# Inverse roots of the norms: a square root on ScalarE and a reciprocal on VectorE in place of a logarithm and an exponential

## The chip, the core and the metric

One core of one Trainium2 chip runs the whole program in one launch. The metric is the device time of an execution in microseconds (us). Engines are named as in the profile: PE is TensorE's matrix multiply and PEld its weight load, DVE is VectorE, ACT is ScalarE, POOL is GpSimd, SP is SyncE, which issues the DMAs.

## What is computed

A sequence of 512 tokens of width 1024 goes through four layers. The first two each hold two branches: an HGRN2 branch (4 heads of 128, chunked gated recurrence) and an RWKV-7 branch (8 heads of 64), merged through gates and an output projection. The last two are a gated linear recurrence (RG-LRU) and a retention layer of 4 heads. Normalisations lie between and inside them. Each needs, per token and group, the inverse root of a mean of squares:

```python
o_hg = o_hg * lax.rsqrt(jnp.mean(jnp.square(o_hg), -1, keepdims=True) + RMS_EPS)   # per HGRN head
y_rw = (y_rw - mu) * lax.rsqrt(var + GN_EPS)                                        # per RWKV head
x = (xf - mu) * lax.rsqrt(var + LN_EPS)                                             # layer norm, twice
y = xf * lax.rsqrt(jnp.mean(xf * xf, axis=-1, keepdims=True) + RMS_EPS)             # RMS norm, four times
out = (out - mu) * lax.rsqrt(var + GN_EPS_2)                                        # per retention head
```

## The kernel before

**Layout.** Activations stand transposed: features on the 128 partitions, the 512 tokens along the columns, so that a width of 1024 is eight tiles of 128x512. Matrix products come close to full fp32 precision by splitting: each activation tile becomes a high part (`act_hi`, a ScalarE copy in `high`, L708) and the rest (`act_lo`, a VectorE subtraction in `low`, L1106), and each block of eight weight tiles a high part (`w_hi`, ScalarE, `weights`, L700) and a low one (`w_lo`, GpSimd, L625). `project` (L1690) then makes three matmuls for every weight tile. Two weight buffers alternate: ScalarE's copy for block b+2 waits until PE has used block b.

**Order of the work.** Every engine's program is written out by hand; engines run their instructions in order and meet at semaphores. Loops of the hardware (`Fori`) run the four HGRN heads of a layer, among others. PSUM banks are shared by a plan of jobs: `job_ready` waits until PE has filled a bank, `job_read` signals that it has been read, `evacuated_job` waits for that signal. A `Chain` counts VectorE's or ScalarE's instructions that have to wait for their own predecessor; in a loop `HG_CHAIN` is the number of such waits per turn.

**Norms.** As tokens lie along the columns, a sum over features is a product with a matrix of ones on PE (`sum_squares`, L1707, or a single matmul), whose result stands on all partitions: one 128x512 tile with a mean of squares for every token. Squares are made by ScalarE (`square`, L715, into two staging tiles, so that from the third on each waits for PE's matmul of the one before the last). Then comes the inverse root, on ScalarE alone:

```python
def inverse_root(dst, job, scale, eps, signal, turn=0):
    x = job_ready(act, job, turn)
    job_read(A(dst, x, ACT.Ln, scale=scale, bias=eps), job)
    evacuated_job(act, job, turn)
    A(dst, dst, ACT.Exp, scale=-0.5).then_inc(signal, 1)
```

VectorE waits for the signal and multiplies (L1109 or L1106). This helper (L720, L722) serves 18 places: the eight HGRN heads (`hg_head`, two layers of four; called at L854), the two layer norms (L960), the four RMS norms (`rms`, L967: `pre0`, `post0`, `pre1`, `post1`), and the four retention heads (L1076). The RWKV group norm of each layer does the same for four tiles at once, four Ln and then four Exp (L935, L938), while VectorE takes them tile by tile: product, gain and bias, bonus, gate, and the split (L1445 to L1452). A table load stands in ScalarE's program wherever the function asked for isn't in the table that is loaded.

**Around the changed places.** Between two HGRN heads ScalarE goes on with the next head's gates (`forget_gate`: two Sigmoids, L810 and L811, and a copy, L813), then the split of the finished head (`high`, L708), then two logarithms (L818, L819), and then a weight copy. VectorE multiplies the head's output by its norm (L1109) and by its gate (L1106), splits it (`low`), and starts on the next head's gates (L1285 on). After the last head both go on to the RWKV chunks, which PE opens by itself. After each retention head but the last two ScalarE's next weight copy comes behind a wait for VectorE's finished products; after the last two the splits come first.

Of the kernel before, what the change touches and what calls it, by code (L numbers as in the profile page):

```python
# [16 lines left out]
ACT = mybir.ActivationFunctionType  # L17

P = 128
T = 512  # L20
D = 1024
# [108 lines left out]

HG_CHAIN = 4

# [169 lines left out]
def build(nc, shapes):  # L302
# [10 lines left out]
    with ExitStack() as ctx:  # L313
        def sb(name, shape, dt=F32):
            return ctx.enter_context(nc.sbuf_tensor(f"{name}_sb", shape, dt))
# [14 lines left out]
        stage = sb("stage", [P, 2, 516])  # L330
        wa = sb("wa", [P, T])
        cond = sb("cond", [P, DEPTH, 24])
        derived = sb("derived", [P, 160])
# [355 lines left out]
        def _(act):  # L689
# [26 lines left out]

            def inverse_root(dst, job, scale, eps, signal, turn=0):

                x = job_ready(act, job, turn)
                job_read(A(dst, x, ACT.Ln, scale=scale, bias=eps), job)  # L720
                evacuated_job(act, job, turn)
                A(dst, dst, ACT.Exp, scale=-0.5).then_inc(signal, 1)  # L722

# [8 lines left out]
            for l in range(DEPTH):  # L732
# [82 lines left out]
                def hg_head(turn, last):  # L815
# [37 lines left out]
                    A(ring[3], x, ACT.Square).then_inc(S("hg_sq"), 1)  # L853
                    inverse_root(scores, ("hg_square", l), 1.0 / P, 1e-6, S("hg_rms"), turn)  # L854
                    if not last:
# [72 lines left out]


                for j in range(QT):  # L930
                    evacuated_job(act, ("gn_mean", l, j))
                    A(R_[:, j, :], P3[:, j, :], ACT.Square).then_inc(S("gn_sq"), 1)
                for j in range(QT):
                    x = job_ready(act, ("gn_var", l, j))
                    job_read(A(K_[:, j, :], x, ACT.Ln, scale=1.0 / 64, bias=64e-5), ("gn_var", l, j))  # L935
                for j in range(QT):
                    evacuated_job(act, ("gn_var", l, j))
                    A(K_[:, j, :], K_[:, j, :], ACT.Exp, scale=-0.5).then_inc(S("gn_rs"), 1)  # L938
                act.wait_ge(block_used, b_gate + 16)
# [12 lines left out]
                for m in range(KT):  # L952
                    weights(b_out + m + 2)
                for m in range(KT):
                    if m < 7:
                        act.wait_ge(S("xc_ready"), 7 * l + m + 1)
                    else:
                        evacuated_job(act, ("ln_mean", l))
                    square(("ln", l), m, xa[:, m, :])
                inverse_root(merged[:, 0, :], ("ln_var", l), 1.0 / D, 1e-5, S("ln_rs"))  # L960


            def rms(key, job, tiles, ready):
                for m in range(KT):
                    ready(m)
                    square(key, m, tiles[:, m, :])
                inverse_root(RS, job, 1.0 / D, 1e-6, S("rms_rs"))  # L967

# [91 lines left out]
            def attend(h):  # L1060
# [9 lines left out]
                for v in range(4):  # L1070
# [4 lines left out]
                    square(("ret", h), v, hg[:, 4 * h + v, :])  # L1075
                inverse_root(RS, ("r_var", h), 1.0 / 512, 1e-5, S("rms_rs"))  # L1076

# [23 lines left out]
        def _(dve):  # L1101
# [9 lines left out]
            def low(n, slot, src, turn=0):  # L1111

                dve.wait_ge(split_hi, n + 1 + turn)
                tt(act_lo[:, slot, :], src, act_hi[:, slot, :].bitcast(F32), ALU.subtract).then_inc(split_lo, 1)

            def spread(ap, n):
# [54 lines left out]
            for l in range(DEPTH):  # L1171
# [105 lines left out]
                with dve.Fori(0, QT) as turn:  # L1277
# [80 lines left out]
                    x = job_ready(dve, ("hg_out", l), turn)  # L1358
                    dve.wait_ge(S("hg_rms"), head + 1)
                    gain = vec[:, bass.ds(vec_at[f"hg_g{l}"][0] + turn, 1)]  # L1360
# [82 lines left out]
                for j in range(QT):  # L1443
                    dve.wait_ge(S("gn_rs"), 4 * l + j + 1)
                    y = P3[:, j, :]  # L1445
                    chain.done(tt(y, y, K_[:, j, :], ALU.mult))
                    chain.done(TS(y, y, V(f"gn_g{l}", j), V(f"gn_b{l}", j), ALU.mult, ALU.add))
# [34 lines left out]
                for m in range(KT):  # L1482
                    evacuated(dve, b_out + m)
                    ins = stt(xa[:, m, :], x, -1.0 / D, xa[:, m, :], ALU.mult, ALU.add)
                    job_read(ins, ("ln_mean", l)) if m == 7 else ins.then_inc(S("xc_ready"), 1)
                dve.wait_ge(S("ln_rs"), l + 1)
                for m in range(KT + 1):
# [7 lines left out]

            def normed(n, pre, count):

                dve.wait_ge(S("rms_rs"), count)
                for m in range(KT):
# [6 lines left out]

            def onto_x(n, post, count, x_in, done):

                dve.wait_ge(S("rms_rs"), count)
                dve.wait_ge(S("x_in"), x_in)  # L1510
# [7 lines left out]

            normed(SPLITS["lru_h"], "pre0", 1)
            with dve.Fori(0, RT // 4) as turn:  # L1520
# [64 lines left out]
            for m in (6, 7):  # L1585
                left(dve, LRU_OUT + m)
            onto_x(0, "post0", 2, 64, S("x_done"))
            dve.wait_ge(S("x_done"), 3 * KT)


            normed(SPLITS["ret_h"], "pre1", 3)

# [19 lines left out]
            def attend(h):  # L1612
# [20 lines left out]
                for v in range(4):  # L1633
                    y = hg[:, 4 * h + v, :]
                    ins = stt(y, x, -1.0 / 512, y, ALU.mult, ALU.add)
                    job_read(ins, ("r_mean", h)) if v == 3 else ins.then_inc(S("ret_c"), 1)
                dve.wait_ge(S("rms_rs"), 4 + h)
                for v in range(4):
# [25 lines left out]
            for m in (6, 7):  # L1664
                evacuated(dve, RET_OUT + KT + m)
            onto_x(1, "post1", 8, 80, S("x_final"))

# [563 lines left out]
```

## Time and profile before

| | us |
|---|---|
| three runs: median (lowest to highest) | 2222.09 (2217.86 to 2224.73) |
| the profiled execution, its own time | 2224.56 |
| its span, first to last instruction | 2222.8 |
| PE busy | 1934.4 |
| VectorE busy | 962.9 |
| ScalarE busy | 869.0 |
| GpSimd busy | 607.8 |

The profiled execution's time is 1.8 us above its span. Its mean granted TensorE clock was 0.955 of full speed. Busy times overlap, and a busy PE is not PE at its peak. In a timeline a row gives the start and the length in us, the engine, the line of the kernel (often that of a helper), the operation with its tiles, and in brackets how long the engine had stood idle and whose end released it.

### The profile page before, as it was taken

To read this page: it belongs to the slowest core of one execution; us is meant where nothing else is said; L and a number is where in the kernel's file an instruction comes from. 1 tells how busy PE (TensorE), PEld (TensorE's weight loads), DVE (VectorE), ACT (ScalarE), POOL (GpSimd) and SP (SyncE) were. 2 spreads that over 40 slices of the span, in tenths; PEclk is the share of its full clock that TensorE was granted. 3 is DMA by queue.
4 is the path that set the end of the run, shared out by engine and by line. 5 is a ranking of instruction groups with operands and counts; after the bars stand their busy time and mean duration, and the time that the engine had idled before them with its cause. 6 is when DMAs were issued, how large, how long until landed. Compare 5 with 4: busy or idle time off the path is not lost.

```text
span 2222.8 us, 35507 instructions
## 1 busy us (share of the span) xinstructions
PE 1934.4 (87%) x14368; PEld 1534.2 (69%) x14368; DVE 962.9 (43%) x1299; ACT 869.0 (39%) x1244; POOL 607.8 (27%) x255
## 2 busy tenths in 40 slices
PE   1999988899787998988899797989597998998987
PEld 1876877798565866877798574865474886777755
DVE  5326375632456126375632434737604123232232
ACT  1333456433323334456433324256515323333322
POOL 0333422200252433422300231422141441322212
PEclk9999999999898999999999899999799999999999
DMA  8232222200364322222200323211132231212112
GB/s 333 84 101 64 93 86 71 67 4 13 127 261 156 104 68 67 90 85 71 67 4 13 133 95 133 95 57 48 61 101 95 95 99 43 86 47 66 56 58 77
DMA packets 57524, 192.80 MB, mean 87 GB/s; under 512 B 5408, under 2 KB 5664, under 8 KB 54976
## 3 DMA queue, kind: packets, MB, share of 16 engines
q1 hardware_dynamic: 57408, 191.10, 25.5%
q8 instruction: 92, 1.51, 0.3%
q14 instruction: 24, 0.20, 0.0%
HBM read 173.25 MB, written 17.83 MB: 86 GB/s over the span
## 4 chain that ended last, share of the span: by engine, by line
issue 51%; PE 29%; POOL 9%; DVE 5%; ACT 3%; DMA 1%; POOLq 0%; DVEq 0%; ACTq 0%; SPq 0%
PE proj L1690 17%; POOL w_lo_sb L625 9%; PE aux L1850 2%; PE aux L1781 2%; DVE area_sb L1106 2%; DMA slots_sb<-w_ada 1%; PE aux L1907 1%; PE proj L1850 1%; PE aux L1904 1%; DVE area_sb L1109 1%; DVE slots_sb L1109 1%; ACT L720 1%; DVE act_lo_sb L1106 0%; DVE slots_sb L1106 0%; ACT L810 0%
## 5 line engine op out<-in xcount | busy, mean ns | idle before, releaser
L625 POOL TENSOR_TENSOR w_lo_sb<-w_raw_sb,w_hi_sb 128x1024 fp32r<-128x1024 f32 x231 | 589.6, 2553 | 1404.1 <-ACT w_hi_sb L700 1404.1
L1690 PE MATMUL proj<-act_hi_sb,w_hi_sb 128*128 128x512 f32 x1784 | 730.3, 409 | 97.4 <-DVE act_lo_sb L1106 63.5
L1690 PE MATMUL proj<-act_lo_sb,w_hi_sb 128*128 128x512 f32 x1784 | 707.3, 396 | 0.0
L1690 PE MATMUL proj<-act_hi_sb,w_lo_sb 128*128 128x512 f32 x1784 | 707.2, 396 | 0.0
L700 ACT ACTIVATE w_hi_sb<-w_raw_sb 128x1024 fp32r<-128x1024 f32 x231 | 244.4, 1058 | 740.4 <-PE proj L1690 687.0
L1690 PEld LDWEIGHTS proj<-act_hi_sb,w_hi_sb 128*128 128x128 f32 x1784 | 343.1, 192 | 192.3 <-issue 63.0
L1690 PEld LDWEIGHTS proj<-act_lo_sb,w_hi_sb 128*128 128x128 f32 x1784 | 343.3, 192 | 74.0 <-issue 6.3
L1690 PEld LDWEIGHTS proj<-act_hi_sb,w_lo_sb 128*128 128x128 f32 x1784 | 342.5, 192 | 74.2
L1106 DVE TENSOR_TENSOR area_sb<-area_sb 128x256 f32<-128x256 f32 (+2 forms) x208 | 141.3, 718 | 20.0 <-ACT area_sb L835 11.8
L1106 DVE TENSOR_TENSOR slots_sb<-slots_sb 128x512 f32<-128x512 f32 (+1 forms) x64 | 73.7, 1155 | 64.1 <-ACT slots_sb L795 26.1
L1106 DVE TENSOR_TENSOR area_sb<-area_sb,slots_sb 128x512 f32<-128x512 f32 (+1 forms) x90 | 72.1, 816 | 49.7 <-ACT slots_sb L722 38.7
L1106 DVE TENSOR_TENSOR slots_sb<-proj,stage_sb 128x512 f32<-128x512 f32 x28 | 19.3, 689 | 167.0 <-ACT stage_sb L1056 143.3
L1707 PE MATMUL aux<-stage_sb,const_sb 128*128 128x512 f32 x128 | 67.4, 667 | 24.3 <-ACT stage_sb L715 24.0
L1109 DVE SCALAR_TENSOR_TENSOR slots_sb<-proj,derived_sb,stage_sb 128x512 f32 x32 | 24.0, 751 | 140.3 <-ACT stage_sb L744 140.3
L1781 PE MATMUL aux<-area_sb 128*128 128x128 f32 x448 | 60.0, 280 | 17.3 <-DVE area_sb L1106 17.3
L1781 PEld LDWEIGHTS aux<-area_sb 128*128 128x128 f32 x448 | 56.7, 191 | 24.5 <-DVE area_sb L1106 20.7
L1850 PE MATMUL aux<-area_sb 64*64 64x64 f32 x1792 | 69.7, 222 | 3.2 <-issue 2.1
L1907 PE MATMUL aux<-area_sb 64*64 64x64 f32 x1280 | 71.5, 218 | 0.6 <-issue 0.4
L1707 PEld LDWEIGHTS aux<-stage_sb,const_sb 128*128 128x128 f32 x128 | 22.5, 205 | 68.2 <-issue 35.8
L1850 PEld LDWEIGHTS aux<-area_sb 64*64 64x64 f32 x1792 | 64.8, 138 | 4.3 <-issue 2.8
L1106 DVE TENSOR_TENSOR slots_sb<-slots_sb,proj 128x512 f32<-128x512 f32 x24 | 16.5, 687 | 111.1 <-ACT slots_sb L947 74.2
L1907 PEld LDWEIGHTS aux<-area_sb 64*64 64x64 f32 x1280 | 63.4, 135 | 1.0 <-issue 0.6
(234 smaller groups left out, 2328.1 us busy)
## 6 DMA issues: line engine op xcount, KB each, us to landing
w_raw_sb<-wall SPq DMA_DIRECT2D x231, 512.0 KB, 3.5
slots_sb<-w_ada SPq DMA_DIRECT2D x8, 1536.0 KB, 7.3
slots_sb<-w_ada SPq DMA_DIRECT2D x8, 1024.0 KB, 5.9
gate_scr<-stage_sb SPq DMA_DIRECT2D x32, 256.0 KB, 2.2
slots_sb<-gate_scr SPq DMA_DIRECT2D x32, 256.0 KB, 4.0
x_scr<-area_sb SPq DMA_DIRECT2D x3, 2048.0 KB, 7.5
area_sb<-x_scr SPq DMA_DIRECT2D x3, 2048.0 KB, 9.5
area_sb<-x_t SPq DMA_DIRECT2D x2, 2048.0 KB, 9.6
```

The costliest lines, as they stand in the source:

```text
L625: nc.gpsimd.tensor_tensor(w_lo[:, b % 2, :, :].rearrange("p k n -> p (k n)"), w_raw[:, b % 2, :], w_hi[:, b % 2, :, :].rearrange("p k n -> ...
L700: A(w_hi[:, b % 2, :, :].rearrange("p k n -> p (k n)"), w_raw[:, b % 2, :], ACT.Copy)\
L720: job_read(A(dst, x, ACT.Ln, scale=scale, bias=eps), job)
L1106: return TT(out_ap, a, b, op)
L1109: return STT(out=out_ap, in0=in0, scalar=scalar, in1=in1, op0=op0, op1=op1)
L1690: ins = MM(bank, w[:, s, k, :], a[:, t, :], start=(start and i == 0), stop=(stop and i == len(terms) - 1))
L1707: ins = MM(x, C("ones"), ST[m % 2], start=(m == 0), stop=(m == tiles - 1))
L1781: ins = MM(x[:, cols], r, r, start=True, stop=True)
L1850: ins = MM(x[q, columns * j:columns * j + columns], a[q, j, :], b(q, j), start=(i == 0), stop=(i == len(products) - 1))
L1904: MM(x[q, 64 * j:64 * j + 64], xt[q, j, :], z[q, j, :], start=True, stop=True)
L1907: ins = MM(x[q, at:at + 64], z[q, j, :], xt[q, j, :], start=True, stop=True)
```

## The change

`inverse_root` becomes `root`, one Sqrt on ScalarE that reads PSUM and signals only that the bank has been read. VectorE waits for that (`inverted`), takes the reciprocal in place, waits for itself, and multiplies as before. `expect_root` is a Sqrt of one column into a tile of its own, called ahead of the squares of the group norms, the layer norms and the RMS norms, so that the table of square roots is loaded there. The HGRN and retention heads have no such call. The semaphores of the old signals go. In the loop of HGRN heads VectorE waits for itself five times a turn, no longer four.

```diff
-HG_CHAIN = 4
+HG_CHAIN = 5
...
-            def inverse_root(dst, job, scale, eps, signal, turn=0):
-
-                x = job_ready(act, job, turn)
-                job_read(A(dst, x, ACT.Ln, scale=scale, bias=eps), job)
-                evacuated_job(act, job, turn)
-                A(dst, dst, ACT.Exp, scale=-0.5).then_inc(signal, 1)
+            def expect_root():
+
+                A(spare[:, :], V("c", 0), ACT.Sqrt, scale=0.0, bias=1.0)
+
+            def root(dst, job, scale, eps, turn=0):
+
+                job_read(A(dst, job_ready(act, job, turn), ACT.Sqrt, scale=scale, bias=eps), job)
...
-                    inverse_root(scores, ("hg_square", l), 1.0 / P, 1e-6, S("hg_rms"), turn)
+                    root(scores, ("hg_square", l), 1.0 / P, 1e-6, turn)
...
+                expect_root()
                 for j in range(QT):
                     evacuated_job(act, ("gn_mean", l, j))
                     A(R_[:, j, :], P3[:, j, :], ACT.Square).then_inc(S("gn_sq"), 1)
                 for j in range(QT):
-                    x = job_ready(act, ("gn_var", l, j))
-                    job_read(A(K_[:, j, :], x, ACT.Ln, scale=1.0 / 64, bias=64e-5), ("gn_var", l, j))
-                for j in range(QT):
-                    evacuated_job(act, ("gn_var", l, j))
-                    A(K_[:, j, :], K_[:, j, :], ACT.Exp, scale=-0.5).then_inc(S("gn_rs"), 1)
+                    root(K_[:, j, :], ("gn_var", l, j), 1.0 / 64, 64e-5)
...
             def rms(key, job, tiles, ready):
+                expect_root()
                 for m in range(KT):
                     ready(m)
                     square(key, m, tiles[:, m, :])
-                inverse_root(RS, job, 1.0 / D, 1e-6, S("rms_rs"))
+                root(RS, job, 1.0 / D, 1e-6)
...
+            def inverted(dst, job, turn=0):
+
+                evacuated_job(dve, job, turn)
+                chain.done(nc.vector.reciprocal(dst, dst))
...
                     x = job_ready(dve, ("hg_out", l), turn)
-                    dve.wait_ge(S("hg_rms"), head + 1)
+                    inverted(scores, ("hg_square", l), turn)
...
                 for j in range(QT):
-                    dve.wait_ge(S("gn_rs"), 4 * l + j + 1)
                     y = P3[:, j, :]
+                    inverted(K_[:, j, :], ("gn_var", l, j))
                     chain.done(tt(y, y, K_[:, j, :], ALU.mult))
...
-                dve.wait_ge(S("ln_rs"), l + 1)
+                inverted(merged[:, 0, :], ("ln_var", l))
...
-                dve.wait_ge(S("rms_rs"), 4 + h)
+                inverted(RS, ("r_var", h))
```

The layer norm and the RMS norms around `normed` and `onto_x` are changed in the same way.

How the instructions move is shown at three places. The first is ScalarE's program at the RWKV group norm of layer 0, before:

```order
L868 ACTIVATE slots_sb<-proj 128x4x64
L932 ACTIVATE slots_sb<-slots_sb 128x512 x4
L935 ACT_TABLE_LOAD
L935 ACTIVATE slots_sb<-aux 128x512 x4
L938 ACT_TABLE_LOAD
L938 ACTIVATE slots_sb<-slots_sb 128x512 x4
L708 ACTIVATE act_hi_sb<-slots_sb 128x512 x4
```

and with the change (the lines have shifted by one to three; L720 is now the one-column root, L724 the root):

```order
L870 ACTIVATE slots_sb<-proj 128x4x64
L720 ACTIVATE spare_sb<-vec_sb 128x1
L935 ACTIVATE slots_sb<-slots_sb 128x512 x4
L724 ACTIVATE slots_sb<-aux 128x512 x4
L709 ACTIVATE act_hi_sb<-slots_sb 128x512 x4
```

Both loads and the four Exps are gone, and no load stands ahead of the one-column root: the last HGRN head has left the table of square roots in place.

The second is VectorE's program for the group norm's first tiles, before:

```order
L1109 SCALAR_TENSOR_TENSOR slots_sb<-aux,slots_sb 128x512 x4
L1106 TENSOR_TENSOR slots_sb<-slots_sb 128x512
L1447 TENSOR_SCALAR slots_sb<-slots_sb,vec_sb 128x512
L1106 TENSOR_TENSOR slots_sb<-slots_sb 128x512 x3
L1447 TENSOR_SCALAR slots_sb<-slots_sb,vec_sb 128x512
L1106 TENSOR_TENSOR slots_sb<-slots_sb 128x512 x2
L1106 TENSOR_TENSOR act_lo_sb<-slots_sb,act_hi_sb 128x512
```

and with the change:

```order
L1110 SCALAR_TENSOR_TENSOR slots_sb<-aux,slots_sb 128x512 x4
L1120 RECIPROCAL slots_sb<-slots_sb 128x512
L1107 TENSOR_TENSOR slots_sb<-slots_sb 128x512
L1453 TENSOR_SCALAR slots_sb<-slots_sb,vec_sb 128x512
L1107 TENSOR_TENSOR slots_sb<-slots_sb 128x512 x2
L1120 RECIPROCAL slots_sb<-slots_sb 128x512
L1107 TENSOR_TENSOR slots_sb<-slots_sb 128x512
L1453 TENSOR_SCALAR slots_sb<-slots_sb,vec_sb 128x512
L1107 TENSOR_TENSOR slots_sb<-slots_sb 128x512 x2
L1107 TENSOR_TENSOR act_lo_sb<-slots_sb,act_hi_sb 128x512
```

Each tile's reciprocal stands ahead of its product, and from the second tile on ahead of the split of the tile before.

The third is ScalarE's program in the loop at the end of an HGRN head, before:

```order
L853 ACTIVATE area_sb<-aux 128x512
L422 REGISTER_ALU
L720 ACT_TABLE_LOAD
L720 ACTIVATE area_sb<-aux 128x512
L722 ACT_TABLE_LOAD
L722 ACTIVATE area_sb<-area_sb 128x512
L810 ISA
L810 ACT_TABLE_LOAD
L810 ACTIVATE area_sb<-area_sb 128x512
```

and with the change:

```order
L855 ACTIVATE area_sb<-aux 128x512
L423 REGISTER_ALU
L724 ACT_TABLE_LOAD
L724 ACTIVATE area_sb<-aux 128x512
L812 ISA
L812 ACT_TABLE_LOAD
L812 ACTIVATE area_sb<-area_sb 128x512
```

Here the root keeps a load of its own right ahead of it, and only the second load and the Exp are gone.

## Rows read from the trace of the kernel before

**Rows 1.** The page: the span, and each engine's busy us, share and instructions.

```profile
span 2222.8 us, 35507 instructions
...
PE 1934.4 (87%) x14368; PEld 1534.2 (69%) x14368; DVE 962.9 (43%) x1299; ACT 869.0 (39%) x1244; POOL 607.8 (27%) x255
```

**Rows 2.** The instructions of line L722: duration ns min/median/max, first and last start.

```profile
L722 ACT ACT_TABLE_LOAD  x18: 1283/1283/1283, 303.1 to 2207.9; - x18
L722 ACT ACTIVATE slots_sb<-slots_sb x10: 629/630/633, 696.9 to 2209.2; 128x512 f32<-128x512 f32 x10
```

**Rows 3.** Timeline between HGRN heads: start, us, engine, line, operation, [idle before].

```profile
302.51 0.60 ACT L720 ACTIVATE area_sb<-aux 128x512 f32<-128x512 f32 x1
...
307.94 0.61 ACT L708 ACTIVATE act_hi_sb<-area_sb  x1
...
305.28 0.75 DVE L1109 SCALAR_TENSOR_TENSOR area_sb<-aux,vec_sb,area_sb 128x512 f32<-128x512 f32 x1 [6.15 <-ACT area_sb L722]
306.20 0.69 DVE L1106 TENSOR_TENSOR area_sb<-area_sb 128x512 f32 x1 [0.17 <-DVE area_sb L1109]
308.73 0.69 DVE L1106 TENSOR_TENSOR act_lo_sb<-area_sb,act_hi_sb  x1 [1.83 <-ACT act_hi_sb L708]
...
316.31 0.50 PE L1690 MATMUL proj<-act_hi_sb,w_hi_sb 128*128 128x512 f32 x1 [1.19 <-POOL w_lo_sb L625]
```

**Rows 4.** Timeline of PE behind layer 0's last HGRN head.

```profile
433.55 1.97 PE L1875 MATMUL aux<-wa_sb,slots_sb 64*64 64x64 f32 x32 [1.74 <-DVE area_sb L1370]
```

**Rows 5.** Timeline around layer 0's group norm, ScalarE, VectorE, then PE.

```profile
553.28 1.28 ACT L935 ACT_TABLE_LOAD   x1
...
557.96 2.19 ACT L938 ACTIVATE slots_sb<-slots_sb 128x512 f32<-128x512 f32 x4
...
558.62 0.69 DVE L1106 TENSOR_TENSOR slots_sb<-slots_sb 128x512 f32<-128x512 f32 x1 [6.02 <-ACT slots_sb L938]
559.35 0.55 DVE L1447 TENSOR_SCALAR slots_sb<-slots_sb,vec_sb 128x512 f32<-128x512 f32 x1
...
570.37 1.47 DVE L1106 TENSOR_TENSOR act_lo_sb<-slots_sb,act_hi_sb 128x512 fp32r<-128x512 f32 x2
...
564.73 0.77 PE L1690 MATMUL aux<-act_hi_sb,w_hi_sb 128*128 128x512 f32 x1 [5.32 <-DVE act_lo_sb L1106]
```

**Rows 6.** Timeline at layer 0's layer norm: the sum of squares, then VectorE's first product.

```profile
684.79 10.07 PE L1707 MATMUL aux<-stage_sb,const_sb 128*128 128x512 f32 x16 [3.55 <-ACT stage_sb L715]
...
697.57 1.29 DVE L1106 TENSOR_TENSOR area_sb<-area_sb,slots_sb 128x512 f32<-128x512 f32 x2 [9.40 <-ACT slots_sb L722]
```

**Rows 7.** Timeline of PE: its waits behind retention heads 0, 2 and 3.

```profile
1876.79 0.50 PE L1690 MATMUL proj<-act_hi_sb,w_hi_sb 128*128 128x512 f32 x1 [0.80 <-POOL w_lo_sb L625]
...
2081.55 0.50 PE L1690 MATMUL proj<-act_hi_sb,w_hi_sb 128*128 128x512 f32 x1 [1.88 <-POOL w_lo_sb L625]
...
2156.42 0.79 PE L1690 MATMUL proj<-act_hi_sb,w_hi_sb 128*128 128x512 f32 x1 [6.00 <-DVE act_lo_sb L1106]
```

**Rows 8.** Timeline ahead of the RMS norm after the recurrent layer, ScalarE and PE.

```profile
1668.74 1.06 ACT L700 ACTIVATE w_hi_sb<-w_raw_sb 128x1024 fp32r<-128x1024 f32 x1 [4.38 <-PE proj L1690]
1669.71 1.13 ACT L715 ACTIVATE stage_sb<-slots_sb 128x512 f32<-128x512 f32 x2
...
1670.46 4.91 PE L1707 MATMUL aux<-stage_sb,const_sb 128*128 128x512 f32 x10 [1.82 <-ACT stage_sb L715]
```

**Rows 9.** VectorE's groups by shape, count | busy us, mean ns | idle before.

```profile
L1106 DVE TENSOR_TENSOR area_sb<-area_sb 128x512 f32<-128x512 f32 x24 | 16.5, 687 | 6.4 <-ACT area_sb L819 6.1
...
L1546 DVE TENSOR_SCALAR slots_sb<-slots_sb 128x512 f32<-128x512 f32 x12 | 5.1, 427 | 0.4
...
L1106 DVE TENSOR_TENSOR derived_sb<-derived_sb 128x4 f32<-128x4 f32 x6 | 1.0, 160 | 0.2
...
L1163 DVE TENSOR_SCALAR derived_sb<-derived_sb 128x4 f32<-128x4 f32 x2 | 0.3, 171 | 0.1
...
L1155 DVE RECIPROCAL derived_sb<-derived_sb 128x4 f32<-128x4 f32 x1 | 0.2, 178 | 0.0
```

More of the change, by code:

```diff
@@ L331, in build @@
         wa = sb("wa", [P, T])
+        spare = sb("spare", [P, 1])
         cond = sb("cond", [P, DEPTH, 24])
@@ L959, in _ @@
                     square(("ln", l), m, xa[:, m, :])
-                inverse_root(merged[:, 0, :], ("ln_var", l), 1.0 / D, 1e-5, S("ln_rs"))
+                root(merged[:, 0, :], ("ln_var", l), 1.0 / D, 1e-5)
             def rms(key, job, tiles, ready):
+                expect_root()
                 for m in range(KT):
@@ L1075, in attend @@
                     square(("ret", h), v, hg[:, 4 * h + v, :])
-                inverse_root(RS, ("r_var", h), 1.0 / 512, 1e-5, S("rms_rs"))
+                root(RS, ("r_var", h), 1.0 / 512, 1e-5)
             ret_blocks(0)
@@ L1494, in _, with normed @@
                 dve.wait_ge(S("x_done"), KT * (l + 1))
-            def normed(n, pre, count):
-                dve.wait_ge(S("rms_rs"), count)
+            def normed(n, pre, job):
+                inverted(RS, job)
                 for m in range(KT):
@@ L1505, in normed, with onto_x @@
                 low(n + 7, 7, ST[1])
-            def onto_x(n, post, count, x_in, done):
-                dve.wait_ge(S("rms_rs"), count)
+            def onto_x(n, post, job, x_in, done):
+                inverted(RS, job)
                 dve.wait_ge(S("x_in"), x_in)
@@ L1516, in onto_x @@
                         tt(xa[:, m - 1, :], xa[:, m - 1, :], OUT[:, m - 1, :], ALU.add).then_inc(done, 1)
-            normed(SPLITS["lru_h"], "pre0", 1)
+            normed(SPLITS["lru_h"], "pre0", "rms_pre0")
             with dve.Fori(0, RT // 4) as turn:
@@ L1586, in _ @@
                 left(dve, LRU_OUT + m)
-            onto_x(0, "post0", 2, 64, S("x_done"))
+            onto_x(0, "post0", "rms_post0", 64, S("x_done"))
             dve.wait_ge(S("x_done"), 3 * KT)
-            normed(SPLITS["ret_h"], "pre1", 3)
+            normed(SPLITS["ret_h"], "pre1", "rms_pre1")
             def ret_blocks(h):
@@ L1665, in _ @@
                 evacuated(dve, RET_OUT + KT + m)
-            onto_x(1, "post1", 8, 80, S("x_final"))
+            onto_x(1, "post1", "rms_post1", 80, S("x_final"))
         @block.tensor
```

## The prediction

> **What bounds the kernel.** I read the page first: TensorE is busy for 1934 of 2223 us, VectorE 963, ScalarE 869 [rows 1]. No engine's sum can pay directly for a change of the norms; what counts is where TensorE stands still because a norm's result is late. So the second view is the timeline around each of the 20 places where an inverse root is taken. At each one a result leaves TensorE, ScalarE makes the root, VectorE multiplies by it and splits the product, and TensorE gets its next operand only then. The third view is the instructions of the helper's second line. Its table load takes 1.28 us and its Exp 0.63 us, 18 times each [rows 2], and VectorE stood idle up to the end of that Exp at most of them ([rows 3]: 6.15 us, [rows 6]: 9.40 us). The norm is thus a serial chain through ScalarE and VectorE with TensorE behind it, and the price of the new chain, stage by stage, is the answer.
>
> **What goes and what comes.** At 18 places the second load, the Exp and its hand-over go; at the two group norms go both loads and the four Exps. In exchange VectorE gets 26 reciprocals of 128x512: 8 for the HGRN heads, 8 for the group norm tiles, 2 layer norms, 4 RMS norms, 4 retention heads. I call the length of one **X** (us) and write every place as a function of it. The square root itself costs what the logarithm did: the same engine and shape, 0.60 us [rows 3].
>
> **X, the one unknown.** The trace has one reciprocal, of 4 columns: 178 ns. A 128x4 TENSOR_TENSOR of the same chain takes 160 ns, and with 687 ns at 512 columns each column of it is worth (687-160)/508 = 1.04 ns over 156 ns fixed [rows 9]. The reciprocal's 18 ns more can be spread over its four columns: 4.5+1.04 = 5.5 ns a column, X = 0.16+512x0.0055 = 3.0 us. Spread over the three steps between four columns it is 7.0 ns, X = 3.8 us. I take the middle, **3.4 us**. If the 18 ns were a fixed cost, X would be near the 0.69 us of the TENSOR_TENSOR, or even the 0.43 us of the fastest 128x512 TENSOR_SCALAR [rows 9]. That is the lower end. In between: the 4-column TENSOR_SCALARs of this stretch take 171 ns [rows 9]; 7 ns over that makes some 2.8 ns a column and 1.6 us. For the upper end see the second rival.
>
> **Place by place**, with waits as the rows have them:
> - Layer norms and the four RMS norms, 6 places. The sum of squares ends at 684.79+10.07 = 694.86, VectorE starts at 697.57 [rows 6]: 2.71 us. Anew: 0.06 to start, 0.60 root, 0.04 hand-over, X, and 0.04 for VectorE's wait on itself (the gap from 559.31 to 559.35 [rows 5]): X+0.74. So each gives **X-1.97**. What the early table brings here is next to nothing: the first load already ran while TensorE summed.
> - Retention heads, 4 places, same chain: X-1.97. All are exposed: behind heads 0 to 2 ScalarE's next weight copy waits for VectorE's products, and TensorE then waits for the low weights, 0.80 us behind heads 0 and 1 and 1.88 us behind head 2; behind head 3 it waits 6.00 us for the split [rows 7]. A gain at heads 0 and 1 could be no more than those 0.80 us; a loss is felt in full.
> - Group norm, 2 places. Now the load starts at 553.28, when the squares are done; the first product starts at 558.62, and TensorE has been waiting 5.32 us at 564.73 [rows 5]. Anew the first root, whose sum is there by then, runs 553.28 to 553.88, its reciprocal to 553.92+X, the product starts at 553.96+X: X-4.66. VectorE has no gap in this stretch up to 571.84 [rows 5], and three more reciprocals with their 0.04 now lie in it: 3X+0.12. Together **4X-4.5**. This is the place that suffers most, since four reciprocals stand in one queue while the four Exps ran beside VectorE's work.
> - HGRN seams between heads, 6 places (three in each layer's loop). The logarithm ends at 303.11, VectorE's product starts at 305.28 [rows 3]. Load and Exp take 1.91 of these 2.17 us, which leaves 0.26 for the hand-over; VectorE's steps in the loop stand 0.17 us apart. Anew 0.26+X+0.17, which is X-1.75. But the split (L708) started only at 307.94, behind the next head's gates on ScalarE, while VectorE was done at 306.89: 1.0 us of slack. So **X-2.75** each, and never better than -1.91 (0.63+1.28), where ScalarE itself sets the split. The next head hangs on this: VectorE's split at 308.73, then its gate chain, then the weight copy and TensorE, which waits 1.19 us at 316.31 [rows 3].
> - Last HGRN heads, 2 places: no next gates, thus no slack. TensorE waits for the product's reading and then for VectorE, 1.74 us at 433.55 [rows 4]: X-1.75.
> - The early tables. The one-column root needs 0.14 us of fixed time (0.60 at 512 columns, 1.06 at 1024 [rows 8]), say 0.2, and a load where another table stands. At the group norms none is needed, at the layer norms ScalarE idled before its first square. Only ahead of the RMS norm after the recurrent layer's output does ScalarE go straight from its last weight copy to the squares, with TensorE waiting 1.82 us for the first one [rows 8]: +1.5 us.
>
> The rest costs nothing: the HGRN and retention roots still get their table late, under the sum of squares, as the logarithm did (1.28 us of load [rows 2]); a Tanh in layer 1 gets a load of its own, and its result is wanted only 17 blocks later.
>
> The sum is 10(X-1.97) + 2(4X-4.5) + 6(X-2.75) + 2(X-1.75) + 1.5 = **26X - 47.2**. It turns from gain to loss at X = 1.82 us. With 3.4 it is +41 us: 2224.6 in the profiled execution becomes 2265.8. That execution stands 2.5 us above the median of the runs, so against the median I say **2263 us**. The readings 3.0 and 3.8 give +31 and +52.
>
> A rule speaks against my pricing of the tables. The trace shows the load at 1.28 us with the Exp directly behind it [rows 2], and one for the logarithm and one for the Exp at every place. By the Trainium skill, ScalarE: Activation LUTs, "What ACT_TABLE_LOAD costs", each switch also costs a drain of about 1.38 us; and its "Table sets" section says one set holds both functions, so that no second load would be needed. By the first every removed switch would be worth 1.38 us more, by the second 1.28 us less. The durations of the rows stand against both, and the sum goes by them.
>
> **Rivals.**
> - *The reciprocal streams* (faster). VectorE makes one column per step, as with a product, and 18 ns is start-up. The place is the same 20 chains; it decides as soon as X is below 1.82 us. With X = 0.69: eight places at -1.28, two at -0.8, group norms 2 x -1.75, seams 6 x -1.91, last heads 2 x -1.06, +1.5 makes -27.5: 2197 profiled, **2195** against the median. For it speaks that 178 ns is near 160; against it, that no other operation of this chain on so few columns comes above 171 ns [rows 9]. Chance 0.08. With X between 1.6 and 2.1 there is no change to be seen: 0.09.
> - *Eight steps a column* (slower still). If the divider holds a column for eight steps of 1.04 ns, X = 0.16+512x0.0083 = 4.4 us, the sum +67 us: **2289**. For four columns it would show 160+3x7x1.04 = 182 ns where the row has 178 [rows 9], so it is not far off. The Trainium skill, VectorE: DVE Perf Modes, in its walkthrough of the pipeline, names this: reciprocal is an iterative divide with a repeat count of 8. The row falls a little short of it. Chance 0.23.
> - *Cover is found* (slower, less). If the seams and retention heads 0 and 1 swallow their loss because TensorE has matmuls left, 6x0.6+2x1.4 = 6.5 us fall away: +34, **2257**. Against it stand the waits of [rows 3, 7]. Chance 0.10.
> - That the early table does nothing is part of the forecast, not a rival: it brings about 0.1 us a place.
>
> My forecast (X from 3.0 to 3.8, everything exposed) has 0.50. The range 2238 to 2293 takes in the forecast, the eight steps and the cover, and reaches down to X = 2.4; it leaves out the two cheap reciprocals, 0.17. A measurement of this kernel can tell 0.3%, 6.7 us, from no change: faster needs X below about 1.6, the time within 0.3% an X up to 2.1. That gives 0.09 faster, 0.08 same, 0.83 slower.
>
> **What would show it.** The profile of the changed kernel should have 26 reciprocals of 3.0 to 3.8 us each; VectorE busy about 88 us more, ScalarE some 45 us less; no load ahead of the group norm's roots; products of that norm some 3.4 us farther apart per tile, with TensorE's second to fourth waits there each over 4 us; the seam of two HGRN heads longer by 0.6 us, not by 3.4. I am wrong if X lies outside 2.4 to 4.5, or if X is as said and the span grows by less than 30 us, which would mean cover at places where I saw waits.

## The result, and the profile after

The changed kernel takes 2259.44 us (median of 4 runs, 2255.26 to 2266.15), the kernel before beside it 2221.18 us. The ratio is 1.0179, with a 95% interval of 1.0159 to 1.0199: slower by 1.8%. The forecast was 2263 us. The profiled execution took 2259.24 us with a span of 2257.5 us, 34.7 us more than before [rows 1].

The head of the page after: VectorE has 88.0 us more, ScalarE 46.6 us less, TensorE nearly the same work.

```profile
span 2257.5 us, 35498 instructions
...
PE 1941.1 (86%) x14368; PEld 1544.3 (68%) x14368; DVE 1050.9 (47%) x1325; ACT 822.4 (36%) x1201; POOL 613.4 (27%) x255
```

The instructions of the two new lines, L1120 (reciprocal) and L724 (root), with duration in ns as min/median/max and the first and last start:

```profile
L1120 DVE RECIPROCAL slots_sb<-slots_sb x18: 3344/3353/3354, 558.2 to 2241.4; 128x512 f32<-128x512 f32 x18
L1120 DVE RECIPROCAL area_sb<-area_sb x8: 3353/3354/3355, 302.5 to 1104.9; 128x512 f32<-128x512 f32 x8
...
L724 ACT ACTIVATE slots_sb<-aux x18: 579/597/600, 557.6 to 2240.6; 128x512 f32<-128x512 f32 x18
L724 ACT ACT_TABLE_LOAD  x11: 1283/1283/1283, 300.6 to 2098.2; - x11
```

So X is 3.35 us, 26 times, where the forecast took 3.4. The root costs 0.60 us as the logarithm did, and a load still stands in front of 11 of the 26 roots: the eight of the HGRN heads and three of the four of the retention heads.

The seam between HGRN heads, which answers to [rows 3], in the timeline after (start, us, engine, line, operation, idle before):

```profile
301.88 0.60 ACT L724 ACTIVATE area_sb<-aux 128x512 f32<-128x512 f32 x1
...
307.88 0.63 ACT L709 ACTIVATE act_hi_sb<-area_sb  x1 [2.42 <-DVE area_sb L1107]
...
302.51 3.35 DVE L1120 RECIPROCAL area_sb<-area_sb 128x512 f32<-128x512 f32 x1 [4.01 <-ACT area_sb L724]
306.02 0.75 DVE L1110 SCALAR_TENSOR_TENSOR area_sb<-aux,vec_sb,area_sb 128x512 f32<-128x512 f32 x1 [0.15 <-DVE area_sb L1120]
306.94 0.69 DVE L1107 TENSOR_TENSOR area_sb<-area_sb 128x512 f32 x1 [0.17 <-DVE area_sb L1110]
...
316.26 0.50 PE L1696 MATMUL proj<-act_hi_sb,w_hi_sb 128*128 128x512 f32 x1 [2.16 <-POOL w_lo_sb L626]
```

The instructions of this trace stood 0.63 us earlier than before's when they came here (the work ahead of the first changed place, which is the same in both). Against that, the product by the root is 1.37 us later (305.28 to 306.02), but the split on ScalarE only 0.57 us (307.94 to 307.88), and the square of the next head comes 0.65 us later. Read who releases the split. Before, the split came when ScalarE was through with the gates; now ScalarE sits idle for 2.42 us and waits for VectorE. The slack that the norm had is used up, and beyond it every tenth counts.

The group norm of layer 0, which answers to [rows 5]:

```profile
557.62 1.07 ACT L724 ACTIVATE slots_sb<-aux 128x512 f32<-128x512 f32 x2
558.93 0.60 ACT L724 ACTIVATE slots_sb<-aux 128x512 f32<-128x512 f32 x1 [0.25 <-PE aux L2025]
...
558.23 3.35 DVE L1120 RECIPROCAL slots_sb<-slots_sb 128x512 f32<-128x512 f32 x1 [1.18 <-ACT slots_sb L724]
561.62 0.69 DVE L1107 TENSOR_TENSOR slots_sb<-slots_sb 128x512 f32<-128x512 f32 x1
...
564.26 3.34 DVE L1120 RECIPROCAL slots_sb<-slots_sb 128x512 f32<-128x512 f32 x1
...
571.12 0.77 PE L1696 MATMUL aux<-act_hi_sb,w_hi_sb 128*128 128x512 f32 x1 [7.27 <-DVE act_lo_sb L1107]
...
577.65 0.80 PE L1696 MATMUL aux<-act_hi_sb,w_hi_sb 128*128 128x512 f32 x1 [4.91 <-DVE act_lo_sb L1107]
...
584.27 0.80 PE L1696 MATMUL aux<-act_hi_sb,w_hi_sb 128*128 128x512 f32 x1 [4.98 <-DVE act_lo_sb L1107]
```

No load stands ahead of the roots. The four tiles of this norm leave VectorE one reciprocal farther apart each, and TensorE waits ahead of the first three. The last two splits come together, so the fourth has no wait of its own, as before.

And the layer norm of layer 0, which answers to [rows 6]: the sum of squares ends at 706.21, the product starts at 710.26, thus 4.05 us where 2.71 us were.

```profile
697.11 9.10 PE L1713 MATMUL aux<-stage_sb,const_sb 128*128 128x512 f32 x16 [5.84 <-ACT stage_sb L716]
...
706.88 3.35 DVE L1120 RECIPROCAL slots_sb<-slots_sb 128x512 f32<-128x512 f32 x1 [6.39 <-ACT slots_sb L724]
710.26 1.29 DVE L1107 TENSOR_TENSOR area_sb<-area_sb,slots_sb 128x512 f32<-128x512 f32 x2
```

The matmuls of a trace of the change can be paired one to one with those of before. What a place costs is how much the later start grows over it (us): at a seam from one head's sum of squares to the next one's, at a group norm up to the third tile's first matmul, elsewhere up to the first matmul that waits for the norm, and at the last norm up to the end of the span. The second profile is that of the last experiment, the same kernel once more:

| place | forecast at X = 3.35 | first profile | second profile |
|---|---|---|---|
| six HGRN seams | 3.6 | 5.8 (0.65, 0.62, 1.6 in layer 0; 0.65, 0.66, 1.6 in layer 1) | 5.3 (0.6, 0.6, 1.4 in each layer) |
| two last HGRN heads | 3.2 | 2.7 (1.4 each) | 2.7 |
| two group norms | 17.8 | 17.4 (8.7 each) | 17.4 |
| layer norms, the norm ahead of the recurrent layer, the last one | 5.5 | 5.4 (1.35 each) | 5.4 |
| the two norms behind the recurrent layer | 2.8 + 1.5 | 6.2 | 4.4 |
| four retention heads | 5.5 | 5.6 (1.4 each) | 5.6 |
| sum | 39.9 | 43.1 | 40.8 |
| elsewhere: TensorE's clock and the work between | 0 | -8.4 | -2.2 |
| span against before | | 34.7 | 38.6 |

### The profile page after: what moved, and what is told of

Its sections match the earlier page's. It is cut to its first block, busy times and chain, and to the rows that moved or that the text cites. A ratio compares the mean times of both kernels' runs of the same rounds, so it can differ in the third digit from the quotient of the medians.

```text
span 2257.5 us, 35498 instructions
## 1 busy us (share of the span) xinstructions
PE 1941.1 (86%) x14368; PEld 1544.3 (68%) x14368; DVE 1050.9 (47%) x1325; ACT 822.4 (36%) x1201; POOL 613.4 (27%) x255
## 4 chain that ended last, share of the span: by engine, by line
issue 67%; PE 15%; POOL 13%; DVE 3%; ACT 1%; POOLq 1%; DVEq 0%; ACTq 0%
POOL w_lo_sb L626 13%; PE proj L1696 6%; PE aux L1856 2%; PE aux L1787 1%; PE aux L1913 1%; PE proj L1856 1%; PE aux L1910 1%; DVE area_sb L1107 1%; DVE area_sb L1120 1%; PE aux L1713 1%; DVE area_sb L1110 0%; POOLq L632 0%; DVE slots_sb L1120 0%; PE proj L1881 0%; PE aux L2157 0%
## 5 line engine op out<-in xcount | busy, mean ns | idle before, releaser
L1120 DVE RECIPROCAL slots_sb<-slots_sb 128x512 f32<-128x512 f32 x18 | 60.3, 3350 | 56.4 <-ACT slots_sb L724 56.4
L1107 DVE TENSOR_TENSOR area_sb<-area_sb,slots_sb 128x512 f32<-128x512 f32 (+1 forms) x90 | 72.1, 816 | 11.2 <-ACT slots_sb L1019 10.1
L1696 PE MATMUL aux<-act_hi_sb,w_hi_sb 128*128 128x512 f32 x64 | 30.2, 472 | 45.3 <-DVE act_lo_sb L1107 34.3
L1856 PEld LDWEIGHTS aux<-area_sb 64*64 64x64 f32 x1792 | 65.1, 138 | 4.4 <-issue 3.2
```

The lines of the kernel that those rows point to most:

```text
L1107: return TT(out_ap, a, b, op)
L1120: chain.done(nc.vector.reciprocal(dst, dst))
L1696: ins = MM(bank, w[:, s, k, :], a[:, t, :], start=(start and i == 0), stop=(stop and i == len(terms) - 1))
L1856: ins = MM(x[q, columns * j:columns * j + columns], a[q, j, :], b(q, j), start=(i == 0), stop=(i == len(products) - 1))
```

## The experiments

Two theories stand. **Length**: every microsecond of a reciprocal is paid at the places as the forecast's formula 26X-47.2 says, so the reciprocal alone decides. **Rivals**: something else carries the 40 us (the early tables, the order of the new chain), or part of the loss is taken back elsewhere. All ratios are to the kernel before on the same chip.

**Half the columns.**

```diff
-                chain.done(nc.vector.reciprocal(dst, dst))
+                chain.done(nc.vector.reciprocal(dst[:, 0:256], dst[:, 0:256]))
```

(and two ScalarE instructions in place of the root, one of which fills the other half with a constant)

> The reciprocals cover 256 of 512 columns; ScalarE writes a constant into the other half, in a second instruction of about 0.2 us more, so tokens 256 to 511 are not normalised. Length theory: X falls from 3.35 us to 0.16+256x0.00624 = 1.76 us; 26 places x 1.59 us = 41 us less than the changed kernel, about 4 us more for the second instruction: 2222, level with the kernel before. Rival (the loss comes from the hand-over to VectorE, its waits on itself and TensorE's lower clock behind them, and not from the instruction's length): the reciprocal count and the waits are unchanged, so 2255 to 2262.

Measured: 2215.67 us, ratio 0.9983 (0.9971 to 0.9995). The groups of VectorE by shape (count | busy us, mean ns | idle before):

```profile
L1122 DVE RECIPROCAL slots_sb<-slots_sb 128x256 f32<-128x256 f32 x18 | 31.5, 1751 | 56.5 <-ACT slots_sb L726 56.5
```

All other parts of the change are in this kernel, and the loss is gone. 256 columns less make 3353-1752 = 1601 ns less: 6.25 ns a column, and 0.15 us fixed. That line gives 0.176 us at 4 columns, where the row of before has 178 ns [rows 9]. The second ScalarE instruction cost less than I had set down for it: at an HGRN head the two take 0.66 us where the one root took 0.60, so under 2 us in all and not 4. The ratio puts this kernel 4 us under before, a little lower than the level that I had expected.

**One reciprocal more at each place**, into a tile that nobody reads.

```diff
+                nc.vector.reciprocal(idle[:, :], dst)
                 chain.done(nc.vector.reciprocal(dst, dst))
```

> Every reciprocal is preceded by a second one into a tile that nobody reads, with no wait between them. Length theory: 26 x 3.35 = 87 us on top of 2259, thus 2346, and the profile shows 52 reciprocals of 3.35 us. Rival (part of the length is covered, since only 38 of the predicted 41 us came): under 2330, with the cover at the seams of the HGRN heads and behind retention heads 0 and 1.

Measured: 2351.2 us, ratio 1.0592 (1.0574 to 1.0609), thus 131 us over before and about 92 over the change. The second of each pair is a little shorter than the first:

```profile
L1121 DVE RECIPROCAL idle_sb<-slots_sb 128x512 f32<-128x512 f32 x18 | 60.3, 3351 | 55.6 <-ACT slots_sb L725 55.6
L1122 DVE RECIPROCAL slots_sb<-slots_sb 128x512 f32<-128x512 f32 x18 | 59.3, 3296 | 0.0
```

The 26 extra ones add 85.6 us of VectorE work and 92 us of time, with some 6 us of uncertainty. The places where the rival had seen cover have none: in this trace each HGRN seam costs 4.3 to 4.5 us and retention heads 0 and 1 cost 4.6 us each, where the change pays 0.6 to 1.6 and 1.4.

**Both group norms back to logarithm and Exp**, the rest as changed.

```diff
-                expect_root()
...
-                    root(K_[:, j, :], ("gn_var", l, j), 1.0 / 64, 64e-5)
+                    job_read(A(K_[:, j, :], x, ACT.Ln, scale=1.0 / 64, bias=64e-5), ("gn_var", l, j))
...
-                    inverted(K_[:, j, :], ("gn_var", l, j))
+                    dve.wait_ge(S("gn_rs"), 4 * l + j + 1)
```

> Only the RWKV group norms go back to logarithm and exponential; the other 18 places keep root and reciprocal. Length theory: the two group norms cost 8.9 us each (4X-4.5), so 17.8 us less than the changed kernel, 2241. Rival (the branch stage behind the group norm has slack that gave 3.1 and 1.6 us back): only 13 us less, 2246. The traces should show it: the shift against the kernel before at the last split tile of the norm and again at the last product of the branch stage.

Measured: 2243.73 us, ratio 1.0115 (1.0089 to 1.0140). The group norms thus account for 0.0064 of the 0.0179, about 14 us, with some 7 us of uncertainty. The time lies between the two expectations and can't tell them apart. The trace can: it moves by 0.01 us over each group norm, and yet the two branch stages behind them are 1.9 and 1.7 us quicker than before. So what those stages give back doesn't hang on the reciprocals ahead of them.

**Without the one-column roots.**

```diff
-                expect_root()
```

> The one-column roots are left out; the table of square roots is then loaded right ahead of each root, while TensorE still sums the squares. Prediction's view: the early table brings 0.1 us a place and costs 1.5 us ahead of the RMS norm behind the recurrent layer: 1 to 2 us less, 2258. Rival (the longer wait there also lowers TensorE's clock in the sum, whose squares stood 1.27 us apart at first instead of 0.86): 3 us less, 2256, and that sum at a granted clock of 1.00 as before. Second rival (the early table is what makes the change bearable): 1.28 us more at 8 places, 2270.

Measured: 2258.46 us, ratio 1.0168 (1.0145 to 1.0191): no difference to the change, and the second rival's 2270 (a ratio of some 1.022) is excluded. The time can't tell the other two expectations, 2258 and 2256, apart. The trace shows what moved. Ahead of the norm behind the recurrent layer, the change has this on ScalarE, and TensorE waits 3.33 us for the first square:

```profile
1690.50 1.28 ACT L720 ACT_TABLE_LOAD   x1
1691.80 0.20 ACT L720 ACTIVATE spare_sb<-vec_sb 128x1 f32<-128x1 f32 x1
1691.91 1.13 ACT L716 ACTIVATE stage_sb<-slots_sb 128x512 f32<-128x512 f32 x2
...
1692.66 9.18 PE L1713 MATMUL aux<-stage_sb,const_sb 128*128 128x512 f32 x16 [3.33 <-ACT stage_sb L716]
```

Without the early root the load sits behind the squares, and TensorE sums them meanwhile. Its wait is the 1.82 us of [rows 8] again:

```profile
1707.94 0.63 ACT L716 ACTIVATE stage_sb<-slots_sb 128x512 f32<-128x512 f32 x1 [0.23 <-PE aux L1710]
1708.59 1.28 ACT L724 ACT_TABLE_LOAD   x1
1709.88 0.60 ACT L724 ACTIVATE slots_sb<-aux 128x512 f32<-128x512 f32 x1
...
1702.07 7.67 PE L1710 MATMUL aux<-stage_sb,const_sb 128*128 128x512 f32 x16 [1.82 <-ACT stage_sb L716]
```

The line L724 has 14 loads there instead of 11, and the three of the early roots are gone. The early table never saves a load; it moves three of them, two to where ScalarE idled and one to where TensorE waits.

**The group norms alone**, on the kernel before.

```diff
-                    job_read(A(K_[:, j, :], x, ACT.Ln, scale=1.0 / 64, bias=64e-5), ("gn_var", l, j))
...
+                    job_read(A(K_[:, j, :], job_ready(act, ("gn_var", l, j)), ACT.Sqrt, scale=1.0 / 64, bias=64e-5), ("gn_var", l, j))
...
+                    inverted(K_[:, j, :], ("gn_var", l, j))
```

> The kernel before with the change in the two group norms alone (eight reciprocals, no one-column roots). By the length of the reciprocal: 4 x 3.35 - 4.5 = 8.9 us at each group norm, of which the branch stages behind took back 3.1 and 1.6 us in the trace of the changed kernel, so 17.8 - 4.7 = about 13 us over before (ratio 1.006). Rival: what was taken back there belonged to the rest of the change, and here the whole 18 us stay (ratio 1.008). Second rival, that parts of the change hide one another: under 6 us.

Measured: 2242.59 us, ratio 1.0091 (1.0071 to 1.0110): 20 us, not 13, and the upper expectation holds. Its trace holds a term that my expectation had left out:

```profile
553.71 1.28 ACT L934 ACT_TABLE_LOAD   x1
555.00 2.07 ACT L934 ACTIVATE slots_sb<-aux 128x512 f32<-128x512 f32 x4
...
555.63 3.35 DVE L1115 RECIPROCAL slots_sb<-slots_sb 128x512 f32<-128x512 f32 x1 [2.60 <-ACT slots_sb L934]
```

Here the HGRN heads leave another table behind, so the load stands between squares and roots. Paired with before, each group norm makes everything 10.1 us later, which is 1.4 more than the 8.7 in the change. Twice 10.1 is the whole 20 us. With the full change the table is there, because the last HGRN head's root drew it; the early root is not needed for it (none of the loads without it falls there).

**The HGRN heads alone**, on the kernel before.

```diff
-                    inverse_root(scores, ("hg_square", l), 1.0 / P, 1e-6, S("hg_rms"), turn)
+                    job_read(A(scores, job_ready(act, ("hg_square", l), turn), ACT.Sqrt, scale=1.0 / P, bias=1e-6), ("hg_square", l))
...
-                    dve.wait_ge(S("hg_rms"), head + 1)
+                    inverted(scores, ("hg_square", l), turn)
```

> The kernel before with the change in the eight HGRN heads alone (root, then a reciprocal on VectorE, HG_CHAIN 5, no early root). By the forecast's prices: six seams at 3.35 - 2.75 = 0.6 us and two last heads at 3.35 - 1.75 = 1.6 us, sum 6.8 us (ratio 1.003). By the shifts of the changed kernel's trace, with one us more where TensorE waited 3.17 us for the product's low part behind head 2: 8 to 9 us. Rival, that a seam's reciprocal hides beside TensorE's gathers: 3 us or less, all of it at the last heads.

Measured: 2225.96 us, ratio 1.0027 (1.0013 to 1.0041), thus 6.0 us for eight reciprocals of 3.35 us, with an interval of 2.9 to 9.1. The forecast's prices say 6.8, and the traces' shifts 8 to 9; this interval can't tell the two apart. In its own trace the first two seams of each layer grow by 0.62 to 0.65 us, the third by 1.5 and 1.3, and the two last heads by 1.4 each, 8.1 us together. So the 2.75 us that the forecast credits a seam are there at four of six. The span grows by 3.0 us only, since TensorE's clock gave back 3.4 us in layer 1's RWKV projections, as it did in the first profile of the change (see the last experiment). The rival with 3 us or less is at the edge of the interval and not excluded by the time alone; the trace excludes it, since the paired starts behind each seam move.

**One instruction for root and inverse.**

```diff
-                job_read(A(dst, job_ready(act, job, turn), ACT.Sqrt, scale=scale, bias=eps), job)
+                job_read(A(dst, job_ready(act, job, turn), ACT.Abs_reciprocal_sqrt, scale=scale, bias=eps), job)
...
-                chain.done(nc.vector.reciprocal(dst, dst))
```

(`HG_CHAIN` is 4 again, and `expect_root` takes the same new function)

> The changed kernel with its square root and reciprocal replaced by one ScalarE instruction, Abs_reciprocal_sqrt; the one-column ones draw its table. VectorE only waits for it: X = 0 in the forecast's sum, which then gives 26 x 0 - 47.2 = 47 us under before, with the floor of 1.91 us at the six seams in place of 2.75 us about 42 us under: some 2177 us, ratio 0.981. Rival, that TensorE takes part of what the places save back at a lower granted clock (its waits shorten at 26 places, its work is the same): 20 to 30 us under, ratio 0.987 to 0.991. Rival, that the roots were never on the path that sets the end and only added work on VectorE counts: no change.

Measured: 2173.73 us (2167.32 to 2177.74), ratio 0.9775 (0.9755 to 0.9796): 45 us under before by the medians, 50 by the ratio. This version beats both kernels. Its group norm, ScalarE, VectorE and TensorE:

```profile
545.97 1.07 ACT L724 ACTIVATE slots_sb<-aux 128x512 f32<-128x512 f32 x2
...
546.58 0.69 DVE L1107 TENSOR_TENSOR slots_sb<-slots_sb 128x512 f32<-128x512 f32 x1 [1.18 <-ACT slots_sb L724]
...
552.70 0.47 PE L1695 MATMUL aux<-act_hi_sb,w_hi_sb 128*128 128x512 f32 x1 [0.47 <-DVE act_lo_sb L1107]
```

The instruction takes the 0.60 us of the square root, VectorE starts 0.61 us after it started, and TensorE waits 0.47 us where it waited 5.32 [rows 5]. Paired with before, everything is 4.83 us earlier over each group norm, and 1.87 to 1.95 us earlier over each HGRN seam: the floor of 1.91, where ScalarE itself sets the split. Over all places, counted as in the table above and without the clock in the sum of squares behind the recurrent layer, it is some 42 us earlier; its span is 46.9 us shorter. The rival that TensorE's clock takes a good part back (20 to 30 us under) falls, and so does the one that only VectorE's added work counts (no change).

**The change once more**, unedited.

> The changed kernel as it is, once more. Its first profile showed TensorE at 0.84 of full speed in the sum of the squares behind the recurrent layer (9.18 us, 7.67 us before), and at 0.88 in the four last products of layer 1's RWKV projections (0.60 before, 3.6 us gained). If these are luck of the clock and not of the code, this profile differs from that one at one of the two places, and the times spread by some us about 2259; if they belong to the code, both stand again.

Measured: 2263.77 us, ratio 1.0187 (1.0163 to 1.0211); its span is 2261.4 us, 38.6 over before. Both places in question turned out otherwise than in the first profile. The last four rows of ScalarE behind layer 1's RWKV projections, first in the first profile of the change:

```profile
831.17 0.69 ACT L768 ACTIVATE slots_sb<-aux,vec_sb 128x512 f32<-128x512 f32 x1 [0.17 <-PE aux L1754]
832.03 0.69 ACT L768 ACTIVATE slots_sb<-aux,vec_sb 128x512 f32<-128x512 f32 x1 [0.17 <-PE aux L1754]
```

They are 0.86 us apart there. Before they were 1.70 us apart:

```profile
820.35 0.69 ACT L766 ACTIVATE slots_sb<-aux,vec_sb 128x512 f32<-128x512 f32 x1 [1.02 <-PE aux L1748]
822.06 0.69 ACT L766 ACTIVATE slots_sb<-aux,vec_sb 128x512 f32<-128x512 f32 x1 [1.02 <-PE aux L1748]
```

In the second profile they are 1.71 us apart again (835.27, 836.98, 838.69). The granted clock was 0.50, the lower level of 1.2 GHz, from 817 to 823.5 us before and from 829 to 841.5 us in the second profile, and 1.00, or 2.4 GHz, from 829 to 833 us in the first. TensorE was busy without a gap in all of these stretches, and its last wait ahead of them was 1.53 us in each of the three traces. And the sum of squares behind the recurrent layer, in the second profile:

```profile
1700.94 7.67 PE L1713 MATMUL aux<-stage_sb,const_sb 128*128 128x512 f32 x16 [3.33 <-ACT stage_sb L716]
```

It took 9.18 us in the first, after the same wait of 3.33 us. So this kernel shows both values at both places, and neither single profile can be read as what the code does. For the sum the code may still have a part in it: in the six traces with the wait of 3.33 us it took 9.2 to 9.3 us three times and 7.67 three times, in the four traces with a wait of 1.82 us (before among them) 7.67 each time. Whether the longer wait makes the slow sum more likely isn't shown by so few.

## Why the prediction was right

**X.** I took 3.4 us from one row of a reciprocal of 4 columns; it measured 3.35. The step that held was to spread the 18 ns by which that row exceeds a product over the columns. The slope is 6.25 ns a column, between the two readings of 5.5 and 7.0, and as long as six of the 1.04 ns in which a product takes a column. The rival of eight steps (4.4 us) falls. With it falls a reading of the Trainium skill, VectorE: DVE Perf Modes, in its walkthrough of the pipeline: the repeat count of 8 that it gives the divide isn't a count of 1.04 ns steps per column here; the measurement decides. That I took the middle was a choice, not knowledge, and that the measured value lay 0.05 us from it was luck; the ends would have given 10 us less or 11 us more.

**The formula.** It has now been measured at four values of X, each against before:

| kernel | X, us | 26X-47.2 | measured by the ratio, us |
|---|---|---|---|
| one instruction | 0 | -47 (-42 with the floor at the seams) | -50 (-54 to -45) |
| half the columns | 1.75 | -2 | -4 (-6 to -1) |
| the change | 3.35 | +40 | +40 (+35 to +44) |
| one more reciprocal | 6.65 | +126 | +131 (+127 to +135) |

The second row leaves out that kernel's second ScalarE instruction, under 2 us by its trace. At X = 0 the retention heads 0 and 1 have a floor too: they gained 1.0 us each, not 1.97.

So the 40 us are the difference of two larger amounts. About 47 us are saved, since loads, Exps and their hand-overs do leave the chain; 87 us of reciprocals take their place, one after another, with TensorE waiting behind nearly all of them. The slope from the change to the doubled one is 27.8 us per us, with 26 at the edge of its uncertainty: in sum nothing is covered. The rival "cover is found" (2257) falls by this and by the traces, where the seams and retention heads 0 and 1 all pay. Its time lies closer to the measured one (2259) than the forecast's 2263: the time alone could not have told the two apart.

**The places.** Group norms cost 8.7 us for 8.9, seams 0.65 for 0.6 at four of six, layer norms and retention heads 1.35 to 1.4 for 1.4. TensorE's waits for the group norm's second and third tile are 4.9 and 5.0 us for "over 4" (there is none for the fourth). VectorE has 88.0 us more for 88, ScalarE 46.6 less for 45. So the mechanism is as forecast.

At the seam, though, the price came out right by two errors that cancel. The hand-over from the root to VectorE takes 0.03 us (302.48 to 302.51), where I had put 0.26, so the product comes 1.37 us later and not 1.6. And the slack was 0.8 us, not 1.0, since the finished product needs 0.25 us to reach ScalarE (307.63 to 307.88), which I had left out. At the last heads, where there is no slack, the first error shows alone: they cost 1.4 us, not 1.6.

**The tables.** Where the load and the Exp left a seam and nothing took their place, in the kernel with one instruction, the seam became 1.87 to 1.95 us shorter: the 1.28 and 0.63 us of the rows. With the drain of 1.38 us that the Trainium skill, ScalarE: Activation LUTs, "What ACT_TABLE_LOAD costs", puts on a switch, it would have been 3.3, an estimate from that figure and the rows. The durations of the rows held.

**What was off.** The third seam of each layer cost 1.6 us instead of 0.6 (1.4 in the second profile of the change, 1.5 and 1.3 with the HGRN heads alone, so it belongs to the code). TensorE waits 3.18 us there for the low weights and the matmuls behind it run at 0.63 us each, the lower clock, up to 406.1 us in the change:

```profile
400.86 0.80 PE L1696 MATMUL proj<-act_hi_sb,w_hi_sb 128*128 128x512 f32 x1 [3.18 <-POOL w_lo_sb L626]
401.45 0.63 PE L1696 MATMUL proj<-act_lo_sb,w_hi_sb 128*128 128x512 f32 x1
...
405.72 0.63 PE L1696 MATMUL proj<-act_hi_sb,w_lo_sb 128*128 128x512 f32 x1
```

Before, the same wait was there, but the clock rose one group of three matmuls earlier:

```profile
399.64 0.61 PE L1690 MATMUL proj<-act_hi_sb,w_hi_sb 128*128 128x512 f32 x1 [3.17 <-POOL w_lo_sb L625]
...
403.03 0.52 PE L1690 MATMUL proj<-act_hi_sb,w_lo_sb 128*128 128x512 f32 x1
```

The other seams lose clock as well. Behind the first one, where TensorE's wait grew from 1.19 to 2.16 us, the mean granted clock from 310 to 330 us was 1.00 before and 0.91 in the change. At the second the matmuls fall back by 1.5 us for this, and a wait of 1.27 us for other work, which stood a little further on before, is gone: the loss is covered there. The forecast had no term for the clock.

All four retention heads pay X-1.97, 1.35 to 1.42 us each in both profiles, as forecast. From root to root they move by 2.9, 0.9, 0.9 and 1.8 us in the first profile and by 1.4, -1.1, 2.4 and 1.3 in the second; what differs lies in the work between the heads and not in the norms. The early table's claims held, with its one price of 1.5 us where no work covered it: TensorE's wait there went from 1.82 to 3.33 us. The two norms behind the recurrent layer cost 6.2 us in the first profile and 4.4 in the second (forecast 4.3), and 1.5 of the difference is the clock in the sum of squares.

Outside the places the first profile of the change is 8.4 us quicker than before, the second 2.2 us. Of the first, 3.6 us are the clock at the RWKV projections. The branch stages behind the group norms give back 3.1 and 1.6 us in the first profile, 3.7 and 2.2 in the second. I first thought that they regularly return part of a loss. But they are quicker than before by 0.2 to 2.5 us in each of the seven other traces too, also where the group norm is unchanged (0.2 and 2.2 with the HGRN heads alone) and where it is faster (2.2 and 1.9 with one instruction). So at least part of it is that the one trace of before was slow in this stage. Its mean granted clock over layer 0's branch stage was 0.91, that of both profiles of the change 0.93, which is too little for all of it. What else sets it stays open.

## What to carry to other kernels

Before moving work from ScalarE to VectorE to save table loads, price the replacement at its full width and by column: at 6.25 ns a column a reciprocal of 512 columns costs more than the load and the second function together (3.35 us against 1.91). In a serial chain every place pays the new instruction in full, and a queue of several on one engine pays several times, as in the group norm. When two steps exist only to build one function, look first whether the engine has that function itself, and how exact it is over your inputs, which no run here shows. And an early table is worth something only if its load would otherwise stand in the chain and ScalarE idles at the new place.

## What the runs showed of the hardware beyond that

- RECIPROCAL of 128 rows in fp32 on VectorE: 0.18 us at 4 columns, 1.75 at 256, 3.35 at 512, five times a product of the same size (0.69 us, [rows 9]).
- Abs_reciprocal_sqrt on ScalarE costs 0.60 us at 128x512, as Sqrt and Ln do, and one load of 1.28 us.
- One program with the same work meets different clocks of TensorE at the same place: the four products at the end of layer 1's RWKV projections took 0.86 us each in one profile of the change and 1.71 us in the other, though TensorE had no gap in either. A difference of 3 to 4 us between two single profiles is within what this clock does by itself.
